# Products whose result nobody reads, placed on TensorE between the output projection and the first expert product

## The reference

```python
coarse = softmax(t @ w_coarse); g_prob, g_idx = top_k(coarse, 1)
fine = (t @ w_fine)[group g_idx]; top_vals, top_idx = top_k(fine, 2)
gates = one_hot(expert_id) * softmax(top_vals) * g_prob
gu = einsum('nd,edf->nef', t, w_up); g_part, u_part = split(gu, 2)
out = einsum('nef,efd->nd', silu(g_part) * u_part * gates, w_down)
x = x + out
```

## Time and profile before

| what | value |
| --- | --- |
| median of 3 runs | 636.18 us (631.79 to 636.21) |
| the profiled execution, its own time | 629.97 us |
| its span, first to last instruction | 628.1 us |
| TensorE busy | 546.0 us, 87% of the span |
| VectorE (DVE) busy | 376.3 us, 60% |
| ScalarE (ACT) busy | 262.1 us, 42% |
| GpSimd (POOL) busy | 199.2 us, 32% |
| mean granted TensorE clock | 0.948 |
| transfers | 102.80 MB, mean 164 GB/s |

### The profile page before, as it was taken

The page is one execution under the profiler, slowest core; times in us unless marked ns, Lnnn a source line. Parts: engine busy times, 40 slices in busy tenths (PEclk is TensorE's granted clock), DMA queues, the critical chain, the costliest instruction groups (busy, mean ns, idle before and its releaser), DMA issues.

```text
span 628.1 us, 7352 instructions
## 1 busy us (share of the span) xinstructions
PE 546.0 (87%) x2589; PEld 426.7 (68%) x2589; DVE 376.3 (60%) x615; ACT 262.1 (42%) x421; POOL 199.2 (32%) x354
## 2 busy tenths in 40 slices
PE   1699799997989979989998799837899999899792
PEld 0488687885777767668887788736677677656550
DVE  3885285775964965865666532378648664664520
ACT  5415125444444354463323221303745755645521
POOL 2549333279288297000000000001123332242211
PEclk9999899999999999899999799756998999999997
DMA  8523520120210301013383722639898999999844
GB/s 304 104 69 109 159 68 6 62 68 1 76 60 12 107 1 43 8 51 110 92 285 134 301 102 112 229 128 300 286 350 258 342 363 358 355 371 351 276 67 68
DMA packets 69219, 102.80 MB, mean 164 GB/s; under 512 B 10528, under 2 KB 42304, under 8 KB 69184
## 3 DMA queue, kind: packets, MB, share of 16 engines
q1 hardware_dynamic: 63184, 80.84, 37.5%
q0 software_dynamic: 4608, 16.78, 10.8%
q10 hardware_dynamic: 1392, 4.74, 1.9%
HBM read 88.71 MB, written 12.58 MB: 161 GB/s over the span
## 4 chain that ended last, share of the span: by engine, by line
PE 57%; DVE 17%; DMA 9%; ACT 7%; POOL 4%; issue 3%; SPq 1%; ACTq 0%; POOLq 0%; DVEq 0%
PE pj L1493 8%; PE pj L1494 7%; PE pj L1495 7%; DMA arena_front<-in_w_expert_up_dram 7%; PE m L1813 7%; PE pj L1791 3%; PE pj L1793 3%; PE pj L1792 3%; PE sc L1570 2%; PE sc L1769 2%; PE tp L1778 2%; ACT arena_back L754 1%; DVE arena_back L1195 1%; ACT arena_back L763 1%; SPq L479 1%
## 5 line engine op out<-in xcount | busy, mean ns | idle before, releaser
L1416 DVE TENSOR_TENSOR up_low<-arena_front,up_high 128x2048 fp32r<-128x2048 f32 x32 | 72.9, 2292 | 44.7 <-ACT up_high L826 44.7
L1493 PE MATMUL pj<-h_high,split 128*128 128x512 f32 x192 | 78.9, 411 | 6.3 <-issue 4.9
L1494 PE MATMUL pj<-h_low,split 128*128 128x512 f32 x192 | 76.5, 399 | 0.0
L1495 PE MATMUL pj<-h_high,split 128*128 128x512 f32 x192 | 76.5, 398 | 0.0
L826 ACT ACTIVATE up_high<-arena_front 128x2048 fp32r<-128x2048 f32 x32 | 60.9, 1914 | 37.2 <-DMA arena_front<-in_w_expert_up_dram 36.3
L604 POOL DMA_INDIRECT out_dram<-arena_back,idx_all x16 | 37.1, 2320 | 104.7 <-DMA out_dram<-arena_back,idx_all 84.0
L1813 PE MATMUL m<-arena_back 128*128 128x512 f32 x128 | 60.7, 619 | 10.6 <-ACT arena_back L838 10.6
L1791 PE MATMUL pj<-up_high,xt_high 128*128 128x512 f32 x128 | 55.3, 432 | 5.3 <-DVE up_low L1416 3.7
L518 POOL TENSOR_TENSOR rstd<-ssq,half_col 128x1 f32<-128x1 f32 x8 | 6.4, 796 | 164.8 <-DVE ssq L945 164.8
L1793 PE MATMUL pj<-up_high,xt_low 128*128 128x512 f32 x128 | 50.6, 395 | 0.0
L1792 PE MATMUL pj<-up_low,xt_high 128*128 128x512 f32 x128 | 50.5, 394 | 0.0
(11 more groups left out here) (314 smaller groups left out, 1207.2 us busy)
## 6 DMA issues: line engine op xcount, KB each, us to landing
arena_front<-in_w_expert_up_dram SPq DMA_DIRECT2D x16, 2048.0 KB, 17.0
arena_back<-in_w_expert_down_dram SPq DMA_DIRECT2D x16, 1024.0 KB, 12.9
arena_front<-in_w_in_dram SPq DMA_DIRECT2D x13, 1024.0 KB, 5.6
arena_front<-in_w_out_dram SPq DMA_DIRECT2D x4, 1024.0 KB, 5.1
arena_back<-in_x_dram SPq DMA_DIRECT2D x4, 512.0 KB, 5.6
arena_front<-in_w_ssm_glu_gate_dram SPq DMA_DIRECT2D x8, 256.0 KB, 2.7
arena_front<-in_w_ssm_glu_val_dram SPq DMA_DIRECT2D x8, 256.0 KB, 3.5
arena_front<-in_w_attn_up_dram SPq DMA_DIRECT2D x8, 256.0 KB, 4.5
```

Of the source, the lines that this page charges most:

```text
L1416: tt(up_low[e4][:, half(h)], ring[e4][:, half(h)], up_high[e4 % 2][:, half(h)].bitcast(F32), ALU.subtract).then_inc(up_low_done, 1)
L1493: pe.matmul(dst, sh, mh, start=first and i == 0, stop=False)
L1494: pe.matmul(dst, sh, ml, start=False, stop=False)
L1495: ins = pe.matmul(dst, sl, mh, start=False, stop=last and i == len(terms) - 1)
```

## The change

A helper issues `n` products of 128 x 512 into `pj[1]`, with the first 128 columns of a held tile as the stationary operand and the whole tile as the moving one. It is called before the prefix sums (14 times a product), before the lists (9), after each of the lists 0 to 7 (2 each), and after the transposes of the first expert's rows (9), which makes 48 by the code. The first three kinds use `m_low`, the last uses `pick[1]`. Nothing reads their result; the next user of `pj[1]`, the second expert's product, starts its sum anew. One wait is added ahead of the first call, for the last residual sum. Nothing is removed or moved.

```diff
             turn_norm2(TT - 1)
             router(TT - 1)
 
+            def keep_busy(n, held):
+
+                for _ in range(n):
+                    pe.matmul(pj[1][:], held[:, 0:P], held, start=True, stop=True)
+
+            pe.wait_ge(x2_done, NOUT * TT)
+            keep_busy(14, m_low[:, 0, :])
             pe.wait_ge(r_pe, 1)
             pe.wait_ge(const_ready, 10)
             flat = lambda i: rt[:, i].rearrange("p t e -> p (t e)")
...
             pe.matmul(mb[0][:, 0:NE], ones[:], cnt[:], start=True, stop=True).then_inc(lg_full, 1)
 
+            keep_busy(9, m_low[:, 0, :])
             pe.wait_ge(route_done, 1)
             def place_lists(lo, hi):
                 for e in range(lo, hi):
                     place_list(e)
+                    if e < LISTS[2]:
+                        keep_busy(2, m_low[:, 0, :])
...
             place_lists(0, LISTS[2])
             turn_rows(0, 0, 16)
+            keep_busy(9, pick[1].rearrange("p t n -> p (t n)"))
             for e in range(4):
                 step(e, e, 0, first=e == 0, lists=e == 3)
```

## The result

Over 22 runs of each kernel the changed kernel takes 636.01 us (median) and the one before 633.24 us. The ratio of changed to before is 1.0057, with a 95% interval of 1.0034 to 1.0080: slower by 3.6 us, between 2.2 and 5.1 (the two medians by themselves lie 2.8 us apart). Single executions scatter widely on both sides (625.87 to 637.43 us before, 629.97 to 639.0 us after), and the two profiled ones happen to be equal: both took 629.97 us, with spans of 628.1 and 628.2 us. What the change costs has to be read inside the profile, from one fixed point to another.

A forecast was written before the change was run, and what follows sets the result against it. TensorE, at half clock in the lists, was taken as the bound there. Terms +4.9 and -1.3 us gave +3.6 us: 639.8 us on the median, 637.1 on the mean, forecast 638.5 us, range 631.5 to 642.5 us.

The forecast's parts named there:

- The first 14: In DVE's routing wait before the prefix product: 6.0 us at half clock, ending at 414.0 us, covered, cost 0.
- The nine before the lists: Between prefix sums and first list: full clock, 2.1 us, ending about 417.5 us, covered, cost 0.
- The sixteen: Between the lists, uncovered: clock falls near the second list's end and stays at half to the lists' end, +4.9 us.
- The last nine and the first expert product: After the row transposes: nine covered, cost 0; they restore the clock, so the first expert product gains, -1.3 us.
- The first two lists: With a pair between them, 1.7 us instead of 1.85 us; the row gather waiting on them moves under 0.2 us.
- Sum: 4.9 - 1.3 = +3.6 us at the first expert product's end, passed whole to the end of the span.
- the idle queues between 450 and 455 us: Transfer share only 0.56 there: transfers wait for slots TensorE frees, so they move by the whole 3.6 us.
- Rival 1: Full clock holds through the lists, six lists at 1.07 us each: -1.1 us, 628.9 us; chance 0.17.
- 0.61 us for a list at full clock: Upper bound for four records of a list; with two added products, 1.07 us at full clock.
- My row of the fall before 401.9 us: Wide, then narrow router products, TensorE busy 1.89 of 2.40 us, clock fell: nearest case for a fall in the lists.
- rival 3: Clock rises again in the list mix or falls later, half the lists at each level: +1.5 us, 631.5 us; chance 0.17.

The follow-up runs named there:

- the run with the idling filled: Changed kernel with 17 products before the lists instead of nine and two more after the second list, pairs kept: 23.41 us from prefix product to first expert product's end.
- the run with four products: Changed kernel with four products after each list instead of two, 14 and nines kept: 26.67 us from prefix product to first expert product's end.
- the narrow run: Changed kernel with 4-column fillers, 26 in first wait, 16 before lists, none between, 15 after transposes: 26.93 us from prefix product to first expert product's end.

## Why the prediction was right

- **The first 14, cost 0.** Right. They end 0.43 us before the prefix product starts, and the clock comes back just before their end.
- **The nine before the lists, cost 0.** Right: full clock, 1.96 us idle left behind them. (By the prediction's own 415.8 + 2.1 us they end at 417.9 us and not at 417.5; either is ahead of the first list.)
- **The sixteen, +4.9 us.** Right in cause and size, and in place to about one list. The clock fell at the end of the first list's pair in one profile and just after the second pair in the other (forecast: near the end of the second list). Lists 2 to 7 took 10.4 us (forecast 10.6 less 0.2), and the clock did not come back in the mix. The expert product starts 23.60 us after the prefix product, where it started 18.73 us after it: +4.87 us. Without the sixteen the loss is gone, with them alone it is 6.0 us.
- **The last nine and the first expert product, -1.3 us.** Right: the product takes 5.54 us against 6.89 us before, and the stretch is 1.37 us shorter when this is done alone.
- **The first two lists.** They took 417.26 to 419.06 us, 1.8 us, near my 1.7; the gather stayed where it was.
- **Sum, +3.6 us on the stretch and at the end.** 3.5 and 3.3 us by the two pairs of profiles, 3.6 us (2.2 to 5.1) by the runs. That the delay reaches the end, as the idle queues between 450 and 455 us said, rests on the timed runs; their interval would also allow for as little as 2.2 us, and in the profiles other turns of the clock cover it. The only part that was not in any row was where executions land: the predicted 638.5 us stands on 634.9 us for the kernel before, 1.7 us above its median over 22 runs, and the medians lie 2.8 us apart, not 3.6. So it is 2.5 us over the measured 636.01.

Rival 1 never happened in the changed kernel, but the run with the idling filled shows its price, and there I was wrong. I took 0.61 us for a list at full clock, from four records at 1.21 / 8 us each, and added a pair to it. In that row DVE's picks set the pace. With pairs between them a list and a pair start 0.91 us apart, not 1.07: the pair fills the wait for the pick. So holding full clock would have been worth about -2.2 us (23.41 against 25.62), not -1.1. My row of the fall before 401.9 us was the right neighbour, though for a reason that I had only half: the run with four products shows the same idling and no fall. I also told that row too weakly: TensorE was busy with wide products and transposes for 11.50 of the 11.50 us up to 399.5 us, and 1.9 us of 20-column products and half a microsecond of idle time behind them were still enough for the fall. In rival 3 a term of 0.4 us stands with no row behind it; as that rival did not occur, no run prices it.

The advice of the Trainium skill, TensorE: Matmul & The Clock Gate, "Why this matters for your kernels", to leave no long idle gaps between bursts, is met in the narrow run, where 22.6 of 25.2 us are busy and no gap is longer than 0.92 us, and the clock stays at half. That it can still help, the run with pairs and no idling suggests: there 1.96 us ahead of the first list were filled, and the clock held. The same page, in "Part 4: PE-mode transpose", says that transposes don't count as busy for the clock in the way that other products do. The traces here leave that open: the clock came back within 0.3 us of the end of these float32 transposes in the run with pairs alone, after 14 us of half clock, and in one profile of the changed kernel, but about 1 us later, in the nine, in the other.

## What to carry to other kernels

Work added only to keep TensorE's clock up belongs into its waits: in front of the first wide product it gave 1.4 us here, between thin products that set the pace at half clock it cost 6. If it must stand on the path, price it at the slower level, and either make sure that the clock holds or leave it out: two products after each list gave a longer stretch than none (29.1 against 23.5 us) and than four (26.7), while with the idle time ahead filled as well, in one execution, they cost next to nothing (23.4). And when executions scatter by 1%, measure from a point that another engine sets to the end of the affected work, and check whether a transfer or gather takes the bound over as soon as the engine gets faster.

## What the runs showed of the hardware

- A TensorE that shows as busy without a break may still get half clock: 10.40 of 10.40 us busy at 0.50 in the changed kernel, and 4.84 of 4.90 us at 0.50 with 4-column products.
- Adding products can shorten the time: with ten more than in the changed kernel the stretch went from 29.1 to 23.4 us (one execution).
- A product of 512 columns costs 0.53 us at half clock when it follows a list (1.06 us a pair) against 0.43 us in a row of its kind, and the list behind it 0.65 us against 0.91 us. At full clock the list behind a pair takes 0.34 us, in the run with pairs and no idling.
- The same program meets the clock's changes at other moments in each execution: the last router took 3.60 us in one profile and 2.52 us in another, and 22 executions of the kernel before lie between 625.87 and 637.43 us, 1.8% apart.
